# Attention of a two-block network on one core: score and value products issued in pairs, each product in its own half of TensorE

## The reference, cut to what matters

```python
# a: 8 heads, 64 + 32 contracted dims, 64 value dims, all 256 keys
p = softmax(q_a @ k_a.T * 96**-0.5);          o_a = p @ v_a
# b: 8 query heads over 2 key/value heads of 64 dims (4 query heads share one)
s = q_b @ k_b.T * 64**-0.5 + bias;  m = max(s, sink)
p = exp(s - m) / (sum(exp(s - m)) + exp(sink - m));   o_b = p @ v_b
# c: 4 heads, each with two 64-dim maps over one 128-dim value
a = softmax(q1 @ k1.T/8 + bias) - lam * softmax(q2 @ k2.T/8 + bias);  o_c = a @ v_c
y = (g0*(o_a*silu(za)) @ w_o_mla + g1*(...) @ w_o_swa + g2*(...) @ w_o_diff) @ w_out
```

## Time and profile before

| | us |
|---|---|
| median of 3 runs | 1977.05 (1975.86 to 1980.72) |
| the profiled execution | 1976.41 |
| its span, first to last instruction | 1974.3 |
| TensorE busy | 1935.1 (98%) |
| VectorE busy | 1216.5 (62%) |
| ScalarE busy | 946.0 (48%) |
| attention units, layer 0 and layer 1 | about 159 to 290 and 472 to 602 |

### The profile page before, as it was taken

One profiled execution on the slowest core, in us unless ns is written; L12 is line 12 of the kernel. 1 busy time (PEld: TensorE's weight loads), 2 busy tenths in 40 slices (PEclk: granted clock), 3 DMA queues, 4 the chain that ended last, 5 costly groups with the idle time before them and its releaser, 6 DMA issues.

```text
span 1974.3 us, 30712 instructions
## 1 busy us (share of the span) xinstructions
PE 1935.1 (98%) x12361; PEld 1597.9 (81%) x12361; DVE 1216.5 (62%) x1782; ACT 946.0 (48%) x1367; POOL 36.1 (2%) x35
## 2 busy tenths in 40 slices
PE   6999999999999999999999999999999999999998
PEld 4999999999999998999999836883588887368833
DVE  4757986666886676666654226961398894059611
ACT  3635563465563475434464205740376673057501
POOL 1000000000000030000000000000000000000000
PEclk7999999999999999999999999999999999999999
DMA  8985465565544543555365899999999999999997
GB/s 289 271 272 172 133 188 153 104 184 173 178 112 132 180 136 101 196 183 176 119 213 189 336 397 405 415 367 405 409 412 409 401 373 349 415 408 411 409 406 293
DMA packets 292565, 536.84 MB, mean 272 GB/s; under 512 B 67076, under 2 KB 198600, under 8 KB 278096
## 3 DMA queue, kind: packets, MB, share of 16 engines
q1 hardware_dynamic: 287968, 530.82, 74.9%
q10 hardware_dynamic: 3920, 3.69, 0.6%
q0 software_dynamic: 544, 0.43, 0.1%
HBM read 533.83 MB, written 1.07 MB: 271 GB/s over the span
## 4 chain that ended last, share of the span: by engine, by line
PE 91%; DMA 5%; DVE 2%; ACT 1%; issue 1%; SPq 0%; DVEq 0%; ACTq 0%
PE bank L811 20%; PE bank L813 20%; PE bank L812 20%; PE bank L1599 9%; PE bank L1626 4%; PE bank L756 3%; DMA pool<-in_od_exp_w 2%; PE bank L982 2%; PE bank L1407 1%; PE bank L771 1%; PE bank L1454 1%; DMA ring<-in_w_ada 1%; PE bank L1483 1%; PE bank L965 1%; DMA ring<-in_w_in 1%; PE bank L951 1%
## 5 line engine op out<-in xcount | busy, mean ns | idle before, releaser
L3113 DVE TENSOR_TENSOR expert_lo<-pool,w_hi 128x2048 fp32r<-128x2048 f32 x168 | 377.0, 2288 | 47.5 <-ACT w_hi L2257 47.4
L2257 ACT ACTIVATE w_hi<-pool 128x2048 fp32r<-128x2048 f32 x168 | 312.9, 1912 | 29.9 <-DMA pool<-in_od_exp_w 25.9
L811 PE MATMUL bank<-h_upper,upper 128*128 128x256 f32 x1056 | 312.9, 296 | 1.7 <-DVE ring_lo L2526 1.3
L812 PE MATMUL bank<-h_lo,upper 128*128 128x256 f32 x1056 | 300.3, 284 | 0.0
L813 PE MATMUL bank<-h_upper,ring_lo 128*128 128x256 f32 x1056 | 300.2, 284 | 0.0
L2526 DVE TENSOR_TENSOR ring_lo<-ring,upper 128x1024 fp32r<-128x1024 f32 x148 | 180.0, 1222 | 99.0 <-ACT upper L1781 98.5
L811 PEld LDWEIGHTS bank<-h_upper,upper 128*128 128x128 f32 x1056 | 203.8, 193 | 4.6 <-issue 2.7
L812 PEld LDWEIGHTS bank<-h_lo,upper 128*128 128x128 f32 x1056 | 204.0, 193 | 1.8 <-issue 0.4
L813 PEld LDWEIGHTS bank<-h_upper,ring_lo 128*128 128x128 f32 x1056 | 203.7, 193 | 0.0
L1599 PE MATMUL bank<-pool,xe_light 128*64 128x512 f32 (+1 forms) x976 | 189.1, 543 | 2.8 <-issue 2.0
L2837 DVE TENSOR_TENSOR piece_lo<-ring,piece_hi 128x1024 fp32r<-128x1024 f32 x118 | 144.8, 1237 | 74.0 <-ACT piece_hi L1770 73.7
(11 more groups left out here) (487 smaller groups left out, 3668.8 us busy)
## 6 DMA issues: line engine op xcount, KB each, us to landing
pool<-in_od_exp_w SPq DMA_DIRECT2D x330, 1024.0 KB, 13.9
ring<-in_w_in SPq DMA_DIRECT2D x48, 1024.0 KB, 5.5
ring<-in_ev_ffn_w SPq DMA_DIRECT2D x33, 1024.0 KB, 5.4
ring<-in_w_ada SPq DMA_DIRECT2D x24, 1024.0 KB, 7.2
ring<-in_od_w_in SPq DMA_DIRECT2D x12, 1024.0 KB, 5.4
ring<-in_ev_w_in SPq DMA_DIRECT2D x10, 1024.0 KB, 5.5
ring<-in_w_in SPq DMA_DIRECT2D x32, 256.0 KB, 4.6
ring<-in_w_out SPq DMA_DIRECT2D x8, 1024.0 KB, 5.0
```

Of the source, the lines that this page charges most:

```text
L811: nc.tensor.matmul(b, left[0], right[0], start=first, stop=False, skip_group_check=True)
L812: nc.tensor.matmul(b, left[0], right[1], start=False, stop=False, skip_group_check=True)
L2257: nc.scalar.activation(w_hi[q % HIS], ring_slot(q), ACT.Copy)\
L3113: V.tensor_tensor(low_slot(q), ring_slot(q), w_hi[q % HIS].bitcast(F32), ALU.subtract)\
```

## The change

**TensorE.** Values of branches a and b are issued for two units at once (`pair_values`): the two products of 64 value columns write the two halves (partitions 0 to 63, 64 to 127) of one bank. Scores of branches b and c are issued for two units at once (`pair_scores`): each contracts 64 rows, one product on rows 0 to 63 and one on rows 64 to 127, into two banks; a pair goes out at every even iteration. The b units come in the order 0, 4, 1, 5, 2, 6, 3, 7, so that a pair has the two key heads. Value pairs of a and b go out at odd iterations, ahead of `turn_probs`. Scores of a, and values of c, stay as they were.

**Other engines.** VectorE gates both halves of a pair in one instruction of 128 rows, and no longer clears key halves. ScalarE copies the b keys once. GpSimd's copies and clears of `kc` go.

```diff
 def units(l):
-    ... + [("b", l, i, True) for i in range(8)] + ...
+    ... + [("b", l, i, True) for i in (0, 4, 1, 5, 2, 6, 3, 7)] + ...
+def valued(br, l, i):
+    return (br, l, i if br == "c" else 2 * (i // 2) + 1 if br == "a" else 4 + i % 4)
...
+def pair_scores(*pair):
+    banks = [claim("attn", ("s", br, l, i), scored, br, l, i) for br, l, i, _ in pair]
+    br, l = pair[0][0:2]
+    pe.wait_ge(proj_ready, when(proj_ready, "kb" if br == "b" else "kc", l, 0 if br == "b" else 3))
+    for t in range(NT):
+        for half, (b, (_, _, i, _)) in enumerate(zip(banks, pair)):
+            r, tok = slice(HEAD * half, HEAD * half + HEAD), slice(P * t, P * t + P)
+            q, k = (qb[r, i % 4, tok], kb[r]) if br == "b" else (qc[r, i // 2, tok], kc[r, i // 2])
+            m = nc.tensor.matmul(b[:, S * t:S * t + S], q, k, start=True, stop=True)
+            if t == NT - 1:
+                m.then_inc(psum_ready, wrote("s", br, l, i))
...
+def pair_values(u, w):
+    br, l, i, _ = w
+    b = claim("attn", ("o", br, l, i), o_ready, br, l, i)
+    pe.wait_ge(probT_ready, when(probT_ready, br, l, i))
+    pe.wait_ge(proj_ready, when(proj_ready, *(("va", l, 1) if br == "a" else ("vb", l))))
+    for k in range(NT):
+        for half, (_, _, j, _) in enumerate((u, w)):
+            at = HEAD * (j if br == "a" else half)
+            m = nc.tensor.matmul(b[HEAD * half:HEAD * half + HEAD, 0:S], (va if br == "a" else vb)[:, k, at:at + HEAD],
+                                 probsT[:, turn_no[br, l, j] % 2, k], start=(k == 0), stop=(k == NT - 1),
+                                 skip_group_check=True)
+    m.then_inc(psum_ready, wrote("o", br, l, i))
 def run_units(us, between, behind):
     for n in range(len(us) + 2):
         if n < len(us):
-            scores(us[n])
+            if us[n][0] == "a":
+                scores(us[n])
+            elif n % 2 == 0:
+                pair_scores(us[n], us[n + 1])
             between(n)
         else:
             behind(n - len(us))
+        if n > 2 and n % 2 and us[n - 2][0] != "c":
+            pair_values(us[n - 3], us[n - 2])
         if 0 < n <= len(us) and us[n - 1][3]:
             turn_probs(us[n - 1])
-        if n > 1 and us[n - 2][3]:
+        if n > 1 and us[n - 2][0] == "c" and us[n - 2][3]:
             values(us[n - 2])
 # ScalarE
-            act.wait_ge(psum_ready, when(psum_ready, "o", *turned[n - 2]))
+            act.wait_ge(psum_ready, when(psum_ready, "o", *valued(*turned[n - 2])))
-        nc.scalar.activation(kb_half(0)[0:HEAD], b[0:HEAD, 0:S], ACT.Copy)
-        nc.scalar.activation(kb_half(1)[HEAD:P], b[HEAD:P, 0:S], ACT.Copy)...
+        copy_out(("kb", l, 0), kb)
 # VectorE, output(u)
-        V.scalar_tensor_tensor(o[br][r, c], b[r, 0:S], 0.5, z[br][r, c], ALU.mult, ALU.mult)
+        V.scalar_tensor_tensor(o[br][:, c], b[:, 0:S], 0.5, z[br][:, c], ALU.mult, ALU.mult)
-        V.memset(kb_half(0)[HEAD:P], 0.0)
-        V.memset(kb_half(1)[0:HEAD], 0.0).then_inc(kb_cleared, tick(kb_cleared, l))
 # GpSimd
-    for l in range(L):
-        pool_engine.wait_ge(psum_ready, when(psum_ready, "o", "a", l, 7))
-        pool_engine.wait_ge(proj_ready, when(proj_ready, "kc", l, 3))
-        G.tensor_copy(kc_odd[HEAD:P], kc[HEAD:P]).then_inc(kc_moved, tick(kc_moved, l))
-        G.memset(kc_odd[0:HEAD], 0.0)
-        pool_engine.wait_ge(kc_moved, when(kc_moved, l))
-        G.memset(kc[HEAD:P], 0.0).then_inc(kc_halves, tick(kc_halves, l))
```

More of the change, by code:

```diff
@@ L252, in k_full @@
         return kn[:, i] if i < 4 else gates[:, 16 + i]
-    kc_odd = va.rearrange("p a b -> p (a b)").rearrange("p (c s) -> p c s", c=4)
-    def kb_half(g):
-        return kb if g == 0 else cq[:, 2]
     subsq = qn
@@ L376, in two_blocks @@
     ada_ready, modsum_ready = sem("ada_ready"), sem("modsum_ready")
-    proj_ready, kb_cleared = sem("proj_ready"), sem("kb_cleared")
-    kc_moved, kc_halves = sem("kc_moved"), sem("kc_halves")
+    proj_ready = sem("proj_ready")
     tanh_ready, modrow_ready, c_in = sem("tanh_ready"), sem("modrow_ready"), sem("c_in")
@@ L595, in units @@
     def units(l):
-        return [("a", l, i, True) for i in range(8)] + [("b", l, i, True) for i in range(8)] + \
+        return [("a", l, i, True) for i in range(8)] + [("b", l, i, True) for i in (0, 4, 1, 5, 2, 6, 3, 7)] + \
                [("c", l, i, i % 2 == 1) for i in range(8)]
@@ L936, in scores @@
             br, l, i, _ = u
[L937 to L946, removed]
@@ L947, in scores @@
-            for t in range(NT):
[L948 to L955, removed]
@@ L956, in scores @@
-            m.then_inc(psum_ready, wrote("s", br, l, i))
+            b = claim("attn", ("s", br, l, i), exp_ready, "exp", br, l, i)
+            pe.wait_ge(rope_ready, when(rope_ready, "q", l, i))
+            pe.wait_ge(proj_ready, when(proj_ready, "kn", l, 3))
+            pe.wait_ge(proj_ready, when(proj_ready, "krows", l))
+            for t in range(NT):
+                m = nc.tensor.matmul(b[:, S * t:S * t + S], q_full(i)[0:HEAD + ROPE, P * t:P * t + P], k_full(i)[0:HEAD + ROPE],
+                                     start=True, stop=True)
@@ L969, in values @@
             br, l, i, _ = u
-            v = {"a": va, "b": vb, "c": vc}[br]
-            at = 0 if br == "b" else P * (i // 2)
-            b = claim("attn", ("o", br, l, i), *((oc_ready, "sq", l, i // 2) if br == "c" else (o_ready, br, l, i)))
+            b = claim("attn", ("o", br, l, i), oc_ready, "sq", l, i // 2)
             pe.wait_ge(probT_ready, when(probT_ready, br, l, i))
[L974 to L979, removed]
+            pe.wait_ge(proj_ready, when(proj_ready, "vc", l, 1))
             pT = probsT[:, turn_no[br, l, i] % 2]
             for k in range(NT):
-                m = nc.tensor.matmul(b[:, 0:S], v[:, k, at:at + P], pT[:, k],
+                m = nc.tensor.matmul(b[:, 0:S], vc[:, k, P * (i // 2):P * (i // 2) + P], pT[:, k],
                                      start=(k == 0), stop=(k == NT - 1))
+            m.then_inc(psum_ready, wrote("o", br, l, i))
[10 more added lines that the diff above has]
+                                         skip_group_check=True)
             m.then_inc(psum_ready, wrote("o", br, l, i))
@@ L2574, in output @@
             br, l, i, _ = u
-            if br == "c":
+            if valued(br, l, i) != (br, l, i) or br == "c":
                 return
-            width, c, row = value_cols(br, i)
+            c = i // 2 if br == "a" else i % 4
             b = psum(dve, "o", br, l, i)
-            r = slice(row, row + width)
-            V.scalar_tensor_tensor(o[br][r, c], b[r, 0:S], 0.5, z[br][r, c], ALU.mult, ALU.mult)\
+            V.scalar_tensor_tensor(o[br][:, c], b[:, 0:S], 0.5, z[br][:, c], ALU.mult, ALU.mult)\
                 .then_inc(o_ready, tick(o_ready, br, l, i))
@@ L2746, in _ @@
                 lower((("zb" + "1" * (c // 2), l), c % 2))
-            dve.wait_ge(proj_ready, when(proj_ready, "va", l, NT - 1))
-            V.memset(kb_half(0)[HEAD:P], 0.0)
-            V.memset(kb_half(1)[0:HEAD], 0.0).then_inc(kb_cleared, tick(kb_cleared, l))
             for c in range(4):
```

3 lines of the change are left out of this document (removed).

## The result

The changed kernel takes 1960.4 us (median of 4 runs, 1959.8 to 1963.0), the kernel before 1976.6 us on the same chip (4 runs, 1975.9 to 1980.7). The ratio is 0.9922, 95% interval 0.9908 to 0.9936: 0.8% faster. The profiled execution took 1960.6 us.

The account below looks back on a forecast made before the run. TensorE was taken to bound both attention stretches. 15.7 - 1.8 - 0.4 = 13.5 us saved gave 1962.9 us profiled, 1963.5 as median; the range ran from 1957 to 1972, with another microsecond on each side.

Parts of the forecast that it names:

- The bound: Both attention stretches: TensorE is busy throughout at full clock, so its savings can reach the end; VectorE a close second.
- Value pairs: Branches a and b: a pair takes 1.22 us instead of 1.74, saving 0.52; 16 save 8.3 us.
- Score pairs: Branches b and c: a pair takes 1.28 us instead of 1.74, saving 0.46; 16 save 7.4 us.
- Loads in the open: Rival at value pairs: weight loads aren't hidden, a pair takes 2.32 us; 1979 us in all, chance 0.03.
- TensorE's sum: Both attention stretches: value and score pairs together save TensorE 15.7 us before new waits.
- New waits (1): First b score pair, iteration 8: waits for ScalarE's exponentials to free a bank, 0.9 us a layer, 1.8 us.
- New waits (2): Branches b and c: every second iteration needs the preceding unit's `scored`; bites only where VectorE is already the bound.
- New waits (3): Layer 0, branch b: VectorE's normalisation lets TensorE save 4.2 us of the 4.6 wanted, so 0.4 us is lost.
- Everything behind only shifts: Behind attention: projections, feed-forward and experts start from TensorE's progress, so a saving shifts all of it.
- VectorE as bound of both layers: Rival in attention: VectorE holds each layer's saving to about 4.2 us, 8.4 us in all; 1968.6 us, chance 0.20.
- No edges: Rival at the pairs: block entry and exit cost vanishes, 0.87 us saved a pair; 19 us, 1958, chance 0.15.
- No overlap: Rivals: score pairs' row halves don't overlap, 1977 us, chance 0.09; or all pairs run one after another, 1989, chance 0.06.

Follow-up runs that it names:

- e6: Changed kernel with ScalarE's copy of the transposes moved ahead of its piece of gate weights: 1957.9 us, ratio 0.9916 to the kernel before.
- e7: Changed kernel with value pairs issued behind the transposes instead of ahead of them: 1958.9 us, ratio 0.9917 to the kernel before.
- e8: Changed kernel with ScalarE's copy ahead of its gate weights' piece and value pairs behind the transposes: 1958.6 us, ratio 0.9916 to the kernel before.
- e2: Changed kernel with values and outputs issued singly as before, so only scores are paired: 1967.5 us, ratio 0.9970 to the kernel before.
- e4: Changed kernel with GpSimd's copy and clears put back on a spare tile, c scores waiting for them: 1960.5 us, ratio 0.9932 to the kernel before.
- e5: Changed kernel run again unedited, as a control: 1960.2 us, ratio 0.9929 to the kernel before.
- e9: Changed kernel with both products of a score pair on rows 0 to 63: 1973.4 us, ratio 0.9982 to the kernel before.
- e10: Changed kernel with both products of a value pair on columns 0 to 63: 1970.4 us, ratio 0.9974 to the kernel before.
- e3: Changed kernel with each pair's loops swapped, all products of one half before the other: 1960.2 us, ratio 0.9937 to the kernel before.

## Why the prediction was right

1963.5 us was forecast, 1960.4 measured. That is inside the whole range (1956 to 1973), and 0.1 us below the narrower band of the forecast itself (1960.5 to 1966.5). 13.5 us were to be saved in attention, and the windows show 13.2. Point by point:

- **The bound.** TensorE in both stretches, clock 1.00: right. What it saved there reached the end. "Without gaps" was not quite so: in the kernel before, the transposes at 213.13 stand 0.15 us behind the normalisation that starts at 211.04 and takes 1.94 us, and that period is 5.20 us instead of 5.07. So VectorE had no lead left there already.
- **Value pairs.** 1.22 us predicted, 1.16 measured; the edge is 0.27 to 0.28 us, not the 0.34 of the earlier trace rows. 0.58 saved a pair, not 0.52.
- **Score pairs.** 1.28 predicted, 1.22 in b and 1.27 in c measured (8.78 less 8.31 is 0.47 saved). The edge that goes with these is 0.35 in b and 0.40 in c. The earlier trace rows gave 0.39 by subtraction; the 0.41 of the sum has no working of its own. The bound of one 128-column load each, 0.09 dearer, didn't show.
- **Loads in the open.** Denied: 8 records of a value pair take 1.01 us from the first start to the transposes, where loads in the open would add 1.1. By the rule of the Trainium skill that was weighed there (TensorE: Matmul & The Clock Gate, Part 3: Packing small matmuls — row/col tiling), a load is hidden only where the row group differs; this trace and the earlier trace rows disagree with it for column halves.
- **TensorE's sum.** 15.7 predicted, 17.2 measured. Both terms were a little too small, since the edges taken from the earlier trace rows were too dear for value pairs and for the score pairs of b.
- **New waits (1), 1.8 us: wrong.** In the kernel after no first b score waited for exponentials. I held their end fixed at 198.06 and let only TensorE move. But they follow from scores and maxima, which moved too. In the kernel after they end at 196.38, and the score pair starts at 197.05. ScalarE in order of time:

```profile
196.18 0.20 ACT L1834 ACTIVATION_READ_ACCUMULATOR sq<-bank,small 128x1 f32 x1
```

  The dependency itself is real: with ScalarE's copy out of the way (e6) it holds TensorE, at 0.2 us instead of 0.9. And a slack read as start less end is 0.10 us too long, since a start that waited comes 0.10 us after the exponentials' end: the 0.26 was 0.16.

- **New waits (2), priced at nothing while VectorE isn't the bound:** no score pair of the kernel after waits for `scored`.
- **New waits (3), 0.4 us: didn't show after.** It showed at 0.4 us in e7 and 0.8 in e8, which ask for the normalisation one value pair earlier, and in e2, where VectorE keeps its 64-row outputs; in e6, which only takes ScalarE's waits away, none is listed. GpSimd's 1.3 us were sized right (e4: 1.4 in the window), on another path. What the dropped `output` instructions give wasn't tried alone.
- **Small pieces ahead of attention, costed at nothing.** The clears on VectorE and the single copy of the b keys weren't tried alone. The part ahead of layer 0 is 0.5 us shorter, inside its spread over the runs (155.5 to 159.3).
- **What was missing: 3.8 us.** "New waits" asked what the score pairs wait for, and not what the moved value pairs wait for. The lost cover, 0.58 us at 187.38, stood in the trace of before. A wait of 2.2 us that doesn't exist stood in place of one of 3.8 that does. That the total came out within 0.3 us is in part luck: the pairs saved 1.5 us more than I had, and the waits cost 1.6 more.
- **Everything behind only shifts.** Right within chance: 3.6 us of the first pair of profiles lie outside attention, and over the runs with the change, or part of it, what lies outside moves by more (1704.2 to 1709.9 us; before 1709.3). By e5's ratio the saving is 14.0 us (0.0071 x 1973.5), by the first 15.4; the windows' 13.2 lies within both intervals.
- **Rivals.** VectorE as bound of both layers: no, it never held TensorE in the kernel after. No edges: no, 0.27 to 0.40 us each. No overlap: no, e9 and e10 show what that would look like, and each gives back 10 to 12 us.

Open: the small gaps behind the late transposes of e2, some 0.5 us, and why the two halves of the change add up to 0.9 us less than the whole.

## What to carry to other kernels

Two f32 matmuls that each fill half of the array cost about one when they sit in different halves, in either order, plus an edge of 0.3 to 0.4 us per block; so pair them where the overlap of a block saves well over that (here 0.87 us). When an instruction is moved ahead in one engine's order, look in the old trace for the end of each of its inputs and subtract: cover that was there by accident (0.58 us here) is spent first. When all of a loop moves earlier, move the releaser in the sum too, not only the one who waits. And where a list of waits names no releaser, compare the start with the ends of its inputs in the rows of all engines: a constant small distance gives the releaser away.

## What the runs showed of the hardware that I had not expected

- f32 pairs in two halves overlap fully even when all products of one half stand ahead of all of the other (e3, 1.07 against 1.06 us for 8 records). The Trainium skill (TensorE: Matmul & The Clock Gate, Part 3: Packing small matmuls — row/col tiling) says that matmuls start and end strictly in program order. An estimate by that rule: the first of the second half's four records would start behind three full ones of the first, 3 x 0.217 = 0.65 us after the pair's start, and end 0.87 later, 1.52 us in all with no edge. The trace of e3 disagrees, as far as the build keeps the program's order, which these rows don't show.
- A start of TensorE that waited comes 0.10 us after the end of ScalarE's instruction (185.83 to 185.93 after, 195.44 to 195.54 in e6) and 0.14 us after the end of VectorE's (235.68 to 235.82 in e2). Slack is what is left beyond that.
- Two kinds of pair next to each other are cheaper than with transposes between them: 0.5 us beyond the wait in layer 1 of e7, over the six places where a score pair follows a value pair, under 0.1 us each; argued from the windows, not tried alone.
- Where nothing was edited, executions differ by up to 1.9 us between the layers and by up to 4.2 us behind them. Between the layers of before and after, 1.6 us apart, the same work ran at mean granted clocks of 0.66 and 0.83. A 1.4 us effect (e4) was plain in a window and invisible in the median of six runs.
